# A two-block transformer kernel on one core: weight sums moved into the last up loop, the start of the second attention reordered, one modulation group summed on VectorE

## The reference

```python
mod = (silu(c) @ ada_w + ada_b)                       # 6 x 1024: sh1, sc1, g1, sh2, sc2, g2
h = rms_norm(x, ln1_g) * (1 + sc1) + sh1
x = x + g1 * (attentions(h @ w_in) @ w_out)           # 4 paired windowed heads x 2 branches, then 4 paired block heads
h = rms_norm(x, ln2_g) * (1 + sc2) + sh2
x = x + g2 * sparse_moe(h)                            # 32 experts, top 4
# second block: 16 meta tokens in front, 272 tokens
h = concat([meta_tokens, x]); hn = rms_norm(h)
q, k, v = split(hn @ sb_w_qkv)                        # 16 heads of 64
z = q @ k.T / 8                                       # causal, strictly
w = exp(log_sigmoid(z) + (reverse_cumsum(-softplus(z)) - (-softplus(z))))
h = h + (w @ v) @ sb_w_o
h = h + mlp(rms_norm(h)); h = h + rglru(rms_norm(h))
h = h + relu(rms_norm(h) @ w_up)**2 @ w_down          # the last mlp
return rms_norm(h)[:, 16:]
```

## Time and profile before

| | us |
|---|---|
| median of 3 runs (lowest to highest) | 1870.19 (1869.49 to 1871.87) |
| the profiled execution | 1869.76 |
| its span, first to last instruction | 1868.0 |
| TensorE matmul busy | 1780.2 (95%) |
| VectorE / ScalarE / GpSimd busy | 547.1 / 261.6 / 121.1 |
| mean granted TensorE clock | 0.996 |

### The profile page before, as it was taken

One profiled execution on the slowest core, in us unless ns is written; L12 is line 12 of the kernel. 1 busy time (PEld: TensorE's weight loads), 2 busy tenths in 40 slices (PEclk: granted clock), 3 DMA queues, 4 the chain that ended last, 5 costly groups with the idle time before them and its releaser, 6 DMA issues.

```text
span 1868.0 us, 21872 instructions
## 1 busy us (share of the span) xinstructions
PE 1780.2 (95%) x8575; PEld 1020.7 (55%) x8576; DVE 547.1 (29%) x1148; ACT 261.6 (14%) x540; POOL 121.1 (6%) x180
## 2 busy tenths in 40 slices
PE   7989999999999899999999898989999999999998
PEld 4546633333333323333333235867888888888787
DVE  2354333223322313323223223133110005612353
ACT  1135211001100001001001002013110001511100
POOL 4604000000000001010010001000000000000000
PEclk9999999999999999999999999999999999999999
DMA  8779899979999999999999998420433343443350
GB/s 322 250 282 285 349 419 428 418 309 430 428 427 429 428 428 428 429 428 428 429 428 428 428 428 313 160 93 33 148 135 135 135 143 134 172 170 135 135 180 23
DMA packets 95493, 547.91 MB, mean 293 GB/s; under 512 B 6002, under 2 KB 9282, under 8 KB 68594
## 3 DMA queue, kind: packets, MB, share of 16 engines
q1 hardware_dynamic: 95442, 547.19, 72.9%
HBM read 546.12 MB, written 1.05 MB: 293 GB/s over the span
## 4 chain that ended last, share of the span: by engine, by line
PE 67%; DMA 27%; DVE 2%; SPq 1%; issue 1%; POOL 1%; ACT 0%; ACTq 0%; POOLq 0%; DVEq 0%
DMA ring<-in_exp_w 27%; PE ps L1289 20%; PE ps L1229 14%; PE ps L1391 6%; PE ps L1441 5%; PE ps L1260 5%; PE ps L905 3%; PE ps L1101 1%; PE ps L1468 1%; PE ps L1183 1%; PE ps L1201 1%; PE ps L877 1%; PE ps L1493 1%; PE ps L1340 1%; PE ps L839 1%
## 5 line engine op out<-in xcount | busy, mean ns | idle before, releaser
L1229 PE MATMUL ps<-ring,arena 128*64 128x512 f32 x2112 | 470.6, 595 | 43.3 <-DMA ring<-in_exp_w 43.2
L1289 PE MATMUL ps<-hn,ring 128*128 128x272 f32 (+1 forms) x1536 | 346.5, 388 | 0.0
L1229 PEld LDWEIGHTS ps<-ring,arena 128*64 128x64 f32 x2112 | 150.0, 137 | 344.2 <-issue 247.7
L1289 PEld LDWEIGHTS ps<-hn,ring 128*128 128x128 f32 x1536 | 291.8, 190 | 53.3
L1260 PE MATMUL ps<-arena,hn 128*64 128x512 f32 x1056 | 233.9, 595 | 3.5
L1260 PEld LDWEIGHTS ps<-arena,hn 128*64 128x64 f32 x1056 | 75.3, 137 | 140.9 <-issue 140.6
L2123 DVE TENSOR_SCALAR sq<-ps 128x512 f32<-128x512 f32 x33 | 22.8, 692 | 345.0 <-PE ps L1229 345.0
L1391 PE MATMUL ps<-arena,ring 128*128 128x272 f32 x512 | 117.6, 393 | 0.5 <-DVE arena L2222 0.5
L1391 PEld LDWEIGHTS ps<-arena,ring 128*128 128x128 f32 x512 | 97.2, 190 | 20.9 <-DVE arena L2222 1.0
L2035 DVE TENSOR_SCALAR sq<-arena,rstd 128x64 f32<-128x64 f32 x68 | 19.2, 325 | 304.3 <-PE ps L1229 303.6
L1619 ACT ACTIVATE sq<-sq 128x512 f32<-128x512 f32 x33 | 20.8, 629 | 531.7 <-DVE sq L2123 531.7
(11 more groups left out here) (388 smaller groups left out, 1531.4 us busy)
## 6 DMA issues: line engine op xcount, KB each, us to landing
ring<-in_exp_w SPq DMA_DIRECT2D x124, 2048.0 KB, 23.0
arena<-in_exp_w SPq DMA_DIRECT2D x67, 2048.0 KB, 21.5
ring<-in_mlp_w_up SPq DMA_DIRECT2D x16, 2048.0 KB, 7.5
ring<-in_mlp_w_down SPq DMA_DIRECT2D x16, 2048.0 KB, 7.7
ring<-in_ada_w SPq DMA_DIRECT2D x8, 2048.0 KB, 8.3
ring<-in_sb_w_qkv SPq DMA_DIRECT2D x6, 2048.0 KB, 14.0
ring<-in_w_in SPq DMA_DIRECT2D x5, 2048.0 KB, 12.5
ring<-in_ada_w SPq DMA_DIRECT2D x8, 1024.0 KB, 9.6
```

The costliest lines, as they stand in the source:

```text
L1229: last = mm(bank(2 + part)[64 * h:64 * h + 64, :], lhs, w[:, k % 2, at:at + 512], start=False, stop=(k == C - 1))
L1289: last = mm(bank((n0 + q) % 8)[:, lo:TT], w[:, k, P * q:P * q + P], act[:, k, lo:TT], start=(k == 0), stop=(k == C - 1))
```

## The change

Four parts.

1. **Modulation group 1 on VectorE.** Its four 2 MB loads move ahead, between the chunks of w_in, and are freed by a new semaphore, mod_added. VectorE multiplies each half's 128 x 2048 rows by the conditioning value of its row and adds them into modacc (add_modulation, eight instructions, after the head norms of chunks 0, 2 and 3); TensorE sums over the rows with one product with ones (modulation_sum, after v = 9) and turns the result after v = 10. The halves of group 2 take the places of group 1 in the compression stage, the other four go into turns 0, 1, 4 and 7 (LATE_PARTS); the score runs a unit ahead: score(u + 1) in turn u. The loads of exp_b1, exp_b2 and cmp_w1 stay behind that of chunk 5 of w_in in the list.
2. **Second attention.** The eight blocks of v are made in banks 4 to 7, four before and four after the first two scores; the turns of v go through banks 6 and 7 and stand between the first units; VectorE and ScalarE place them by turns.
3. **Weight sums** of slots 0 and 1 run in turns 23 to 30 of the up loop.
4. **The last of the four stores** is issued by ScalarE.

```diff
-           + [("ada", group, k) for group in (1, 2) for k in range(4)] + [("wout", 0, h) for h in range(2)])
+           + [("in", 0, 1), ("in", 0, 2), ("ada", 1, 0), ("ada", 1, 1), ("in", 0, 3), ("ada", 1, 2), ("in", 0, 4),
+              ("ada", 1, 3), ("in", 0, 5), ("cmp", 0, 0)] + [("ada", 2, k) for k in range(4)] + [("wout", 0, h) for h in range(2)])
 A_CMP, A_N = A_LOADS.index(("cmp", 0, 0)), len(A_LOADS)
+LATE_PARTS = (0, 1, 4, 7)
 MOD_BANK, MOD_TURN_BANK = (6, 7, 7), (5, 7, 7)
 B_LOADS = ([("qkv", 0, c) for c in range(6)] + [("wo", 0, c) for c in range(2)]
@@ -130,6 +131,8 @@
     kind, layer, c = A_LOADS[n]
     if (kind, c) == ("in", 0):
         return "in_first", 1
...
         return "chunk_done", N_GIN1 - 1 + 4 * (c - 1)
     first = {"qkv": N_QKV, "wo": N_WO, "lin": N_LIN, "lout": N_LOUT, "up": (N_UP0, N_UP1)[layer]}[kind]
     return "chunk_done", first + 4 * (c + 1)
...
         if kk == 1:
             last.then_inc(s["mod_parts"], 1)
+    def modulation_sum(group):
+        pe.wait_ge(s["mod_added"], 4)
+        for r in range(4):
+            last = mm(bank(MOD_BANK[group])[32 * r:32 * r + 32, :], m.ones[:, 0:32], m.modacc[:, 512 * r:512 * r + 512],
+                      start=True, stop=True)
+        last.then_inc(s["mod_parts"], 4)
...
+        if v == 9:
+            modulation_sum(1)
+        elif v == 10:
+            turn_modulation(1)
...
     for u in range(UNITS + 3):
-        if u < UNITS:
-            if u == 0:
-                pe.wait_ge(s["cmp_dve"], CMP_DVE.index("exp_in") + 1)
-            if u >= 2:
-                pe.wait_ge(s["maxed"], u - 1)
-            score(u)
         if u == 0:
-            modulation_half(1, 4)
-            modulation_half(1, 5)
-        elif u < 3:
-            modulation_half(1, 5 + u)
-        elif u == 3:
-            turn_modulation(1)
-        elif u < UNITS:
-            modulation_half(2, u - 4)
-        elif u == UNITS:
+            pe.wait_ge(s["cmp_dve"], CMP_DVE.index("exp_in") + 1)
+            score(0)
+        if u + 1 < UNITS:
+            if u >= 1:
+                pe.wait_ge(s["maxed"], u)
+            score(u + 1)
+        if u in LATE_PARTS:
+            modulation_half(2, 4 + LATE_PARTS.index(u))
+        elif u == UNITS - 2:
             turn_modulation(2)
         if u == UNITS + 2:
...
-    for c in range(6):
+    for c in range(4):
         dense(N_QKV + 4 * c, B_QKV + c, m.hn, made=("b_h_ready", 0) if c == 0 else None,
               waits=projection_waits(0, c, "chunk_dve", 0, sum_before=3))
-    pe.wait_ge(s["b_consts"], 1)
-    pe.wait_ge(s["chunk_dve"], 24)
-    for n in range(6):
+    def project_values(c):
+        w = b_slot(B_QKV + c)
+        for q in range(4):
+            pe.wait_ge(s["chunk_dve"], 4 * c + q - 3)
+            for k in range(C):
+                last = mm(bank(4 + q)[:, 0:TT], w[:, k, P * q:P * q + P], m.hn[:, k, :], start=(k == 0), stop=(k == C - 1))
+            last.then_inc(s["chunk_done"], 1)
+    def turn_values(n):
         t, h = n // 2, n % 2
         rows = min(P, TT - P * t)
         for q in range(4):
-            last = turn(bank(n)[0:rows, P * q:P * q + P], m.bv[:, 4 * h + q, P * t:P * t + rows], ident)
+            last = turn(bank(value_bank(n))[0:rows, P * q:P * q + P], m.bv[:, 4 * h + q, P * t:P * t + rows], ident)
         last.then_inc(s["v_turned"], 1)
...
+    project_values(4)
+    pe.wait_ge(s["b_consts"], 1)
+    pe.wait_ge(s["chunk_dve"], 16)
     b_score(0)
     b_score(1)
-    for i in range(9):
-        if i < 8:
+    project_values(5)
+    pe.wait_ge(s["chunk_dve"], 22)
+    b_score(2)
+    pe.wait_ge(s["b_sp"], 1)
+    b_accumulate(0)
+    pe.wait_ge(s["chunk_dve"], 24)
+    turn_values(0)
+    turn_values(1)
+    pe.wait_ge(s["b_sp"], 2)
+    b_accumulate(1)
+    pe.wait_ge(s["v_placed"], 2)
+    turn_values(2)
+    turn_values(3)
+    pe.wait_ge(s["b_w"], 1)
+    b_score(3)
+    pe.wait_ge(s["v_placed"], 4)
+    turn_values(4)
+    turn_values(5)
+    pe.wait_ge(s["b_sp"], 3)
+    b_accumulate(2)
+    pe.wait_ge(s["v_placed"], 6)
+    b_weigh(0)
+    for i in range(2, 9):
+        if 2 < i < 8:
             pe.wait_ge(s["b_sp"], i + 1)
             b_accumulate(i)
-        if i >= 1:
-            pe.wait_ge(s["b_w"], i)
-            if i >= 3:
-                pe.wait_ge(s["b_o_copied"], i - 2)
-            b_weigh(i - 1)
+        pe.wait_ge(s["b_w"], i)
+        if i >= 3:
+            pe.wait_ge(s["b_o_copied"], i - 2)
+        b_weigh(i - 1)
         if i + 2 < 8:
             b_score(i + 2)
...
-    for i in range(8):
+    soft(2)
+    def place_values(n):
+        t, h = n // 2, n % 2
+        rows = min(P, TT - P * t)
+        act.wait_ge(s["v_turned"], n + 1)
+        copy(m.vtok[0:rows, t, 512 * h:512 * h + 512], bank(value_bank(n))[0:rows, :], "v_placed")
+    def b_weights(i):
         act.wait_ge(s["b_summed"], i + 1)
         if i >= 2:
             act.wait_ge(s["b_o_done"], i - 1)
         q = 2 * (i % 3)
         f(m.w[:, i % 2], m.ps[:, q:q + 2, 0:432], ACT.Exp).then_inc(s["b_w"], 1)
+    place_values(1)
+    b_weights(0)
+    place_values(3)
+    b_weights(1)
+    place_values(5)
+    soft(3)
+    for i in range(2, 8):
+        b_weights(i)
         if i + 2 < 8:
             soft(i + 2)
...
+    def add_modulation(part):
+        r, amount = A_AT[A_LOADS.index(("ada", 1, part))]
+        dve.wait_ge(s.loaded[r], amount)
+        w = m.ring[:, r, :].rearrange("p (k n) -> p k n", n=2048)
+        for k in range(2):
+            cond = m.condR[:, 2 * part + k, 0:1]
+            if part == 0 and k == 0:
+                last = v.tensor_scalar(m.modacc, w[:, k, :], cond, None, ALU.mult)
+            else:
+                last = v.scalar_tensor_tensor(m.modacc, w[:, k, :], cond, m.modacc, ALU.mult, ALU.add)
+            if k == 0:
+                link(last)
+        last.then_inc(s["mod_added"], 1)
+        dve.wait_ge(s["mod_added"], part + 1)
...
+        for part in {0: (0, 1), 2: (2,), 3: (3,)}.get(c, ()):
+            add_modulation(part)
+        if c == 3:
+            modulation_rows(1)
+        elif c == 4:
+            modulation(1)
...
     for u in range(UNITS + 2):
-        if u == 3:
-            modulation_rows(1)
-        elif u == 4:
-            modulation(1)
-        elif u == 5:
...
-        elif u == UNITS:
+        elif u == UNITS - 3:
             modulation_rows(2)
-        elif u == UNITS + 1:
+        elif u == UNITS - 1:
             modulation(2)
...
-    for n in range(24):
+    def projected(n):
         dve.wait_ge(s["chunk_done"], n + 1)
-        src = bank(n % 8)[:, 0:TT]
+        src = bank(n % 8 if n < 16 else 4 + n % 4)[:, 0:TT]
         if n < 8:
             last = v.scalar_tensor_tensor(m.bq[:, n, :], src, DH ** -0.5, m.rstd[:], ALU.mult, ALU.mult)
         elif n < 16:
@@ -2175,11 +2258,13 @@
         else:
             last = v.tensor_tensor(m.bv[:, n - 16, :], src, m.rstd[:], ALU.mult)
         last.then_inc(s["chunk_dve"], 1)
...
+    for n in range(20):
+        projected(n)
     clamped(0)
     clamped(1)
+    projected(20)
     softplus(0)
-    for i in range(8):
-        if i + 1 < 8:
+    projected(21)
+    softplus(1)
+    projected(22)
+    projected(23)
+    clamped(2)
+    place_values(0)
+    softplus(2)
+    place_values(2)
+    clamped(3)
+    place_values(4)
+    head_output(0)
+    for i in range(2, 8):
+        if i < 7:
             softplus(i + 1)
-        if i >= 1:
-            head_output(i - 1)
+        head_output(i - 1)
         if i + 2 < 8:
             clamped(i + 2)
     head_output(7)
@@ -2399,10 +2497,8 @@
                                ALU.mult).then_inc(s["b_relu"], 1)
...
-    for n in range(4):
-        weight_sums(0, n)
-    for n in range(4):
-        weight_sums(1, n)
+        if n >= 23 and n < 31:
+            weight_sums((n - 23) // 4, (n - 23) % 4)
...
-                sp.wait_ge(s["out_ready_act"], t + 1)
-                sp.dma_start(out[0, P * t:P * t + P, 512:D], m.out_tok[:, t, 512:D]).then_inc(s["out_stored"], 16)
+            sp.wait_ge(s["out_ready_act"], 1)
+            sp.dma_start(out[0, 0:P, 512:D], m.out_tok[:, 0, 512:D]).then_inc(s["out_stored"], 16)
...
+            act.wait_ge(s["out_ready_act"], 2)
+            act.dma_start(out[0, P:2 * P, 512:D], m.out_tok[:, 1, 512:D]).then_inc(s["out_stored"], 16)
```

More of the change, by code:

```diff
@@ L132, in a_freed @@
         return "in_first", 1
+    if (kind, layer) == ("ada", 1):
+        return "mod_added", c + 1
     return {"mod": ("mod_parts", c + 1), "ada": ("mod_parts", 4 * layer + c + 1), "in": ("z_done", 2 * (c + 1)),
@@ L165, in b_freed, with value_bank @@
     return "chunk_done", first + 4 * (c + 1)
+def value_bank(n):
+    return 6 + n % 2
 def first_token(norm_number):
@@ L406 @@
 prm_turned prm_ready sig_ready cond_ready x_turned x_placed squared norm_summed root_ready
-mod_parts mod_rows mod_turned mod_ready h_ready
+mod_parts mod_added mod_rows mod_turned mod_ready h_ready
```

(9 more changed lines are left out.)

7 lines of the change are left out of this document (4 added, 3 removed).

## The result

| | before | after |
|---|---|---|
| median (lowest to highest), us | 1871.03 (1869.49 to 1872.01) | 1851.65 (1851.19 to 1852.48) |
| profiled execution / its span | 1869.76 / 1868.0 | 1852.04 / 1850.4 |
| mean granted clock | 0.996 | 0.997 |

The change makes the kernel faster: the ratio of the times is 0.9898, interval 0.9881 to 0.9915, that is 19.4 us by the medians and 17.6 by the two spans. 1853.7 was forecast with the range 1850 to 1861, so total and range hold. Term by term it is less tidy. This is the ledger: where the same piece of work starts in the trace, in us.

A forecast was written before the change was run, and what follows sets the result against it. TensorE was taken to bound first attention, with its waits in second attention and the last mlp; -5.8 - 6.4 - 3.8 - 0.45 = -16.45 from 1869.76 gave 1853.3, with the median's 0.4 1853.7 us, range 1850 to 1861.

The forecast's parts named there:

- The loop, -8.4: First attention's loop: eight halves, four transposes and an earlier last score leave TensorE; 8.4 us gained, bounds 5 and 10.2.
- The 1.3 and 0.5: First attention's loop: 1.3 us lost to ScalarE's order and 0.5 to the router's weight product on VectorE.
- The w_in stage, +1.4 and +0.9: w_in stage: modulation_sum and four transposes cost 1.4 us; chunk 3 of w_in lands 0 to 1.8 late, 0.9 taken.
- GpSimd beside the compression chain, +0.3: Compression chain: GpSimd's splitting of the biases moves later and runs beside VectorE there; 0.3 us lost (0 to 1).
- The adds at nothing: w_in stage: VectorE's eight adds take 20 to 22 us within 37 us before v = 9, costing nothing.
- The rival of late adds: w_in stage: GpSimd stretches the adds to 48 us, TensorE stands about 17 us at v = 9; 1870.7 us, 4%.
- The front in all, -5.8: All of part 1, w_in stage through first attention: 5.8 us gained, bounds -8.8 and 0, passed on one to one.
- the front gives nothing: Part 1: the loads or ScalarE's order return its whole gain; 1859.5 us, 14%.
- Second attention, -6.4: Second attention's start: three waits of 4.94 us and a slow accumulate's 1.46 us go; 6.4 us gained.
- Up loop, -3.8: Last mlp: the 3.79 us wait for weight sums goes whole, no relu late; 3.8 us gained (-3.8 to -3.0).
- Store, -0.45: End of the kernel: two queues save one store issue; 0.45 us gained (-0.9 to +0.5).
- The clock in the first attention: First attention: gaps in every turn drop TensorE to 1.2 GHz, up to 26 us more; 1879.7 us, 4%.

The follow-up runs named there:

- the late turn: The kernel after, with modulation group 2's turn and its VectorE part moved two units later, behind first attention's scores: median 1850.19 us, ratio to before 0.9896.
- the part alone: The kernel before with only the change's front (modulation group 1 on VectorE, scores a unit ahead, rearranged units): ratio to before 0.9973.
- 7.3 alone: The kernel before with only the rearrangement of second attention's first units: ratio to before 0.9946.
- 5.9 alone: The kernel before with only the edit of the up loop's weight sums: ratio to before 0.9959.
- two others: The kernel before with only the change's front, and with only second attention's rearrangement: ratios to before 0.9973 and 0.9946.

## Why the prediction held, step by step

- **The loop, -8.4.** Measured 7.5 to 8.0 in five profiles with the same loop (from first scores to w_out 43.18 twice, 42.98, 42.97 and 42.67, against 50.71). The size is near, the way to it was not right. The sum began with 10.2, of which 1.9 were for the last score standing a turn earlier. But TensorE stood idle for only 1.50 us in the whole loop of before, and a score that is moved is still work to be done, so that there were no 1.9 us to win; the upper bound of 10.2 could not be reached (8.36 of work and 1.50 idle are 9.9). The 1.3 and 0.5 that were taken off again hid this: what is left is by luck the work taken out, 8.4. Of it, 0.9 went to new idle time. That includes a wait of 1.75 us, some 0.8 of it (the gain of the late turn) with a cause that I had not in view: a turn of the modulation ahead of a flip. Its 0.59 us on TensorE and two instructions on VectorE stand in the chain that the shorter loop made critical. w_out started at 173.00 and not about 171.
- **The w_in stage, +1.4 and +0.9.** The sum and the turn 1.43. The late chunk was within its bounds of 0 to 1.8 in every profile, 1.52 in the one compared, 0.8 in the mean. A further 0.5 us is spread over the matmuls of this stage in after (49.38 us of its own products against 48.91 in before) and was not followed up.
- **GpSimd beside the compression chain, +0.3.** Not seen: from the first transposes to the first scores 19.79 us against 19.85.
- **The adds at nothing.** 18.1 us in all (1.28 + 16.8), where 20 to 22 were reckoned; they end at 89.98, VectorE then waits 5.03 us for TensorE's sum. The rival of late adds needed 48 us. The slowest add took 2.74 us instead of 2.35, 1.16 times and not the 2.3 of the earlier trace rows. It began beside a copy of GpSimd, which ended at 59.75; the next one ran beside a memset from its start to 63.62 and took 2.35. So GpSimd at work is not in itself what slows an add. The timelines of VectorE and GpSimd in after (the two adds stand together above, as 5.12):

```profile
59.16 2.74 DVE L1914 SCALAR_TENSOR_TENSOR arena<-ring,arena 128x2048 f32<-128x2048 f32 x1 [0.43 <-DMA ring<-in_ada_w]
61.93 2.35 DVE L1914 SCALAR_TENSOR_TENSOR arena<-ring,arena 128x2048 f32<-128x2048 f32 x1
57.78 1.97 POOL L652 COPY arena<-arena 128x512 f32<-128x512 f32 x2 [5.89 <-ACT arena L1556]
61.82 1.80 POOL L657 MEMSET arena<- 32x2048 bf16 x1
```

- **The front in all, -5.8.** 4.0 at w_out in the compared pair (4.5 at q, k, v), 5.3 (5.8) with the part alone; the difference is mostly the late chunk (1.52 us against none). The expert stage passed each on, as forecast: the rival "the front gives nothing" falls.
- **Second attention, -6.4.** 7.1 in the ledger, 7.3 alone. Waits of 4.94 and 1.55 us for the slow accumulate are right; some 0.6 us more went with the reordering and are not split up.
- **Up loop, -3.8: the term that was mis-sized.** "The wait of 3.79 us goes whole" is right, and so is that no relu is late; but the same step that gave the second attention its 1.46 us for the clock behind a wait was not made here, though this wait is the longer one. Measured 5.7 (3.95 + 1.76), 5.9 alone. The price of the clock was 1.8 us in one profile of the old wait and 2.9 in two others.
- **Store, -0.45.** 0.2: an issue on SP was counted whole, and about half of it reached the end.
- **The clock in the first attention.** It fell ahead of the loop as in before (0.50 from 130 to 134, in before from 126 to 130) and was back at 1.00 from 136 on; the window from 150 to 175 shows 1.00, with 22.77 us busy of 25. The rule on transposes that spoke against the change did not show. In all five of these loops the first turns ran at half the clock for some time, and for how long differs; most of the 0.5 us between 43.18 and 42.67 lies there (7.92 and 7.46 us to the first flip).

The errors have both signs: the front 1.3 to 1.8 us too hopeful in the compared pair, the second attention and the up loop 2.7 too careful together. That the total came within 2.1 us is in part luck: the places of the gains were forecast right, the errors of their sizes cancel. The lower bound of 1850.3 took the second attention at 6.4; with its own bound of 6.6 it would be 1850.1, which changes nothing.

## What to carry to other kernels

A wait of TensorE costs more than its length where the granted clock halves behind it: look at the windows behind every longer wait, and count that with the wait. Where the wait can't be taken away, harmless products in it buy the clock back, as long as they don't overrun it (read in a trace how long one takes first: here it was twice what was reckoned). Moving work that stays on the same engine gains no more than that engine's idle time, so sum up the idle time first. When a loop gets shorter, go through what was left in it unchanged: a small step ahead of a flip became its longest wait. And a piece of the chain on another engine is no idle time of this one.

## What had not been expected of the hardware

- Behind the waits of 2.73 and 3.79 us the granted clock was 0.50 for some 3 to 6 us; behind that of 1.75 us in the attention's loop, and behind that of 1.52 for w_in's chunk, it stayed at 1.00. The same wait of 3.79 us cost 1.8 us in one profile and 2.9 in others.
- The first add, with one tensor as its source, takes 1.28 us for 2048 float32 elements a partition, and the others, with two, 2.35. The Trainium skill (VectorE: DVE Perf Modes, Mode 2×_2P — use both read ports for one tensor) says that an operation with a single source can use both read ports for it and so give two results a cycle; the trace agrees, 1.8 times.
- The issue of a store takes ScalarE 0.40 us and SyncE 0.36 to 0.45.
